# Moving the per-layer-embedding product of a hybrid block into its routing step, and unrolling the last stage

## The reference

```
h  = x + mixers(rmsnorm(x, g_mix)) @ w_out            # delta rule + convolution
h  = h + moe(rmsnorm(h, g_moe))                       # 64 experts in 8 groups, top 2, F = 256
gate = sigmoid(rmsnorm(h, g_ple) @ w_ple_gate)        # [T, D] @ [D, D]
h  = h + gate * (p @ w_ple_proj)                      # [T, 256] @ [256, D]
out = rmsnorm(h, g_final)
```

## Time and profile before

| | us |
|---|---|
| median of three runs (lowest, highest) | 1401.87 (1398.05, 1403.14) |
| the profiled execution's own time | 1394.22 |
| its span, first to last instruction | 1392.4 |
| PE busy in the span | 1149.8 (83%) |
| DVE busy | 623.1 (45%) |
| ACT busy | 314.4 (23%) |
| moved by DMA | 272.81 MB, 208 GB/s over the span |

### The profile page before, as it was taken

One profiled execution on the slowest core, in us unless ns is written; L12 is line 12 of the kernel. 1 busy time (PEld: TensorE's weight loads), 2 busy tenths in 40 slices (PEclk: granted clock), 3 DMA queues, 4 the chain that ended last, 5 costly groups with the idle time before them and its releaser, 6 DMA issues.

```text
span 1392.4 us, 17070 instructions
## 1 busy us (share of the span) xinstructions
PE 1149.8 (83%) x6357; PEld 761.7 (55%) x6358; DVE 623.1 (45%) x906; ACT 314.4 (23%) x685; POOL 248.3 (18%) x347
## 2 busy tenths in 40 slices
PE   6999899995888886998188878888887888838997
PEld 5888788874777775887033333323332333317775
DVE  5799899964745745322711111111111111154553
ACT  5212111134543434221010101001010000032232
POOL 4000100023564441000212111111211111011111
PEclk9999999997978998999589999999999988979998
DMA  6111121100000103211989999999799999961221
GB/s 200 31 46 32 51 55 46 46 1 0 2 1 1 62 2 114 92 64 57 368 324 425 424 424 421 418 409 383 316 421 424 424 423 415 374 241 55 99 98 45
DMA packets 68066, 272.81 MB, mean 196 GB/s; under 512 B 12521, under 2 KB 38314, under 8 KB 51370
## 3 DMA queue, kind: packets, MB, share of 16 engines
q1 hardware_dynamic: 56096, 254.33, 46.1%
q0 software_dynamic: 9456, 16.80, 3.2%
q10 hardware_dynamic: 2458, 0.92, 0.3%
HBM read 264.15 MB, written 25.43 MB: 208 GB/s over the span
## 4 chain that ended last, share of the span: by engine, by line
DMA 24%; PE 19%; DVE 3%; issue 2%; ACT 1%; SPq 1%; POOL 0%; POOLq 0%; ACTq 0%; DVEq 0%
DMA wup<-in_w_up_dram 20%; PE ps_u L2236 10%; PE ps_gate L94 5%; DMA qkvT<-in_w_ple_proj_dram 2%; PE ps_y L2257 2%; DMA xg<-xn_rows,gi 1%; PE ps_xg L2225 1%; PE ps_hT L2484 1%; PE ps_u L2280 1%; DMA convT<-y_rows 0%; DVE hn L2429 0%; DVE qkvT L2422 0%; DMA y_rows<-qkvT,si 0%; SPq L1707 0%; DVE hn L2453 0%
## 5 line engine op out<-in xcount | busy, mean ns | idle before, releaser
L2236 PE MATMUL ps_u<-wup,xgT 128*64 128x512 f32 x1024 | 259.1, 664 | 63.2 <-DMA wup<-in_w_up_dram 60.8
L2236 PEld LDWEIGHTS ps_u<-wup,xgT 128*64 128x64 f32 x1024 | 86.3, 152 | 234.7 <-issue 233.5
L94 PE MATMUL ps_b<-n_hi,wh 128*128 128x512 f32 x384 | 157.3, 410 | 0.6 <-DVE wl L418 0.6
L94 PE MATMUL ps_b<-n_lo,wh 128*128 128x512 f32 x384 | 151.8, 395 | 0.0
L94 PE MATMUL ps_b<-n_hi,wl 128*128 128x512 f32 x384 | 151.8, 395 | 0.0
L2156 DVE TENSOR_TENSOR hb<-sil,ps_u 128x256 f32<-128x256 f32 x32 | 13.5, 420 | 304.1 <-ACT sil L2096 304.1
L94 PEld LDWEIGHTS ps_b<-n_hi,wh 128*128 128x128 f32 x384 | 73.3, 191 | 16.5 <-issue 2.5
L94 PEld LDWEIGHTS ps_b<-n_hi,wl 128*128 128x128 f32 x384 | 73.0, 190 | 16.2
L94 PEld LDWEIGHTS ps_b<-n_lo,wh 128*128 128x128 f32 x384 | 73.1, 190 | 15.0 <-issue 1.0
L461 DVE SCALAR_TENSOR_TENSOR convT<-upad,vecT,convT 128x1024 f32<-128x1024 f32 (+1 forms) x75 | 79.6, 1061 | 0.0
L2096 ACT ACTIVATE sil<-ps_u 128x256 f32<-128x256 f32 x32 | 12.3, 383 | 291.7 <-PE ps_u L2236 291.7
(11 more groups left out here) (365 smaller groups left out, 1973.8 us busy)
## 6 DMA issues: line engine op xcount, KB each, us to landing
wup<-in_w_up_dram SPq DMA_DIRECT2D x64, 2048.0 KB, 18.6
zT<-in_w_down_dram SPq DMA_DIRECT2D x32, 1024.0 KB, 18.7
convT<-in_w_down_dram SPq DMA_DIRECT2D x32, 1024.0 KB, 19.9
wraw<-in_w_in_dram SPq DMA_DIRECT2D x24, 512.0 KB, 4.3
convT<-y_rows SPq DMA_DIRECT2D x16, 512.0 KB, 4.7
qkvT<-in_x_dram SPq DMA_DIRECT2D x8, 512.0 KB, 8.5
qkvT<-in_w_out_dram SPq DMA_DIRECT2D x8, 512.0 KB, 5.1
xr<-in_x_dram SPq DMA_DIRECT2D x8, 512.0 KB, 3.3
```

The source lines that it names most:

```text
L94: ins = nc.tensor.matmul(ps, lhs[a], rhs[b], start=first and k == 0, stop=last and k == 2)
L2236: last = nc.tensor.matmul(ps_u[k][HC[c], :], xgT[k][:, j, HC[c]], wup[k][c][:, j, :], start=j == 0, stop=j == NJ - 1)
```

## The change

1. **Loads.** In the output-product block SP, once `w_out` is split, also loads all of `p` (1 MB, to `qkvT` slots 10 and 11) and `w_ple_proj` (1 MB, slots 8 and 9).
2. **The product of p** is done in the routing block, in float32, without a split: two transposes and 2 x 2 matmuls of 512 columns for each of 8 tiles. It is laid around PE's three jobs: tiles 0 and 1 before `ps_tot`, tiles 2 to 4 and half of tile 5 before `ps_tab`, the rest after it. ACT copies each tile's turned rows and its result out of PSUM and stores the result (512 KB) to DRAM as `pp_rows`. Tiles 2 to 5 leave through `convT`, so SP waits for their stores before it fetches the second pair's down weights.
3. **End of the experts' block.** `w_ple_gate` alone is left (8 pieces). Five are split here; `silu` of pair 31 now comes before the third split on ACT, and `hidden(1)` and `hidden_turned(1)` before the third on DVE. The scatter of pair 31 and pieces 5 to 7 go to the final block. SP no longer waits for the scatters here; it fetches two tiles of `pp_rows`.
4. **Final block.** All 8 tiles are written out, without a loop. The product of `p` is gone; its rows come from `pp_rows`. Four tiles of experts' rows are asked for at the start, in two pairs of buffers, and tile t + 4 after that. On DVE `add_experts(t + 2)` stands right after `scale(t + 1)` at the step's start, and the output of tile t moves into the next step.

```diff
# output-product block, SP
+                sp.wait_ge(s_wo_lo, NJ)
+                sp.dma_start(p_all, p[0, 0].rearrange("(t q) d -> q t d", q=P)).then_inc(s_pin, 16)
+                sp.dma_start(wpp, w_ple_proj[0].rearrange("(j q) n -> q j n", q=P)).then_inc(s_pin, 16)
...
# routing block, SP
+                    if k:
+                        sp.wait_ge(s_pps, 16 * (NT - 4))
                     for c in G2:
                         fetch_down(sp, k, c, NPR * c + k)
...
# routing block, ACT
+                def p_out(t):
+                    act.wait_ge(e_pp, t + 1)
+                    nc.scalar.activation(ppo[t], ps_pp[t % 2][:].rearrange("p h n -> p (h n)"), ACT.Copy).then_inc(e_out, 1)
+                    act.wait_ge(e_out, t + 1)
+                    act.dma_start(pp_rows[t * P:(t + 1) * P, :], ppo[t]).then_inc(s_ppe if t < 2 else s_pps if t < NT - 2 else s_ppl, 16)
...
# routing block, PE
+                def p_half(t, h):
+                    for j in range(NJP):
+                        last = nc.tensor.matmul(ps_pp[t % 2][:, h, :], pT[t % 2][:, j, :], wpp[:, j, HF[h]], start=j == 0, stop=j == NJP - 1)
...
+                p_products(0, 2)
                 pe.wait_ge(s_iota, 9)
                 pe.wait_ge(s_rv, at["ohs"])
...
+                p_products(2, 5)
+                p_turn(6)
+                p_product(5)
                 pe.wait_ge(s_rv, at["onehots"])
...
+                p_half(5, 1)
+                p_products(6, NT)
...
# end of the experts' block, ACT (DVE alike)
                 result(0, p, 16 * i)
-                for j in range(2, N_X + 2):
+                silu(1, p + 1)
+                for j in range(2, N_E):
                     weights_high(j)
-                silu(1, p + 1)
                 result(1, p + 1, 16 * i)
-                for j in range(N_X + 2, NWJ):
-                    weights_high(j)
...
# final block, DVE
+                for j in range(N_E, NWJ):
+                    weights_low(j)
+                add_experts(0)
+                add_experts(1)
                 dve.wait_ge(s_gfin, 32)
+                scale(0)
+                low(0)
+                for t in range(NT):
+                    if t + 1 < NT:
+                        scale(t + 1)
+                    if t + 2 < NT:
+                        add_experts(t + 2)
+                    if t:
+                        scaled_out(t - 1)
+                    gated(t, 0)
+                    if t + 1 < NT:
+                        low(t + 1)
+                    gated(t, 1)
+                    add_gated(t)
+                scaled_out(NT - 1)
...
# final block, PE
+                    pe.wait_ge(f_lo, t + 1)
+                    product(t, 0)
+                    if t + 1 < NT:
+                        transposes(t + 1)
+                    product(t, 1)
...
# final block, SP
+                for t in range(NT + 1):
+                    if t + 4 < NT:
+                        sp.wait_ge(f_y2, t + 3)
+                        fetch_rows(sp, t + 4, t % 2)
+                    if t:
+                        sp.wait_ge(f_out, t)
+                        sp.dma_start(out[0, (t - 1) * P:t * P, :], ho[(t - 1) % 2]).then_inc(s_fo[(t - 1) % 2], 16)
+                    if t + 2 < NT:
+                        sp.wait_ge(f_m1, t + 1)
+                        fetch_ple(sp, t + 2, t % 2)
```

More of the change, by code:

```diff
@@ L2017, in _ @@
                 fetch_pairs(MID, NIT - 1)
-                for j in range(NWJ):
+                for j in range(N_E):
                     if j >= NRAW:
@@ L2393, in _, with gate @@
-                over_tiles(act, step)
+                    nc.scalar.activation(hx[t % 2][0][:], ps_h[:], ACT.Copy).then_inc(f_hi, 1)
+                def gate(t, h):
+                    act.wait_ge((f_g0, f_g1)[h], t + 1)
+                    nc.scalar.activation(hn[t % 2][:, HF[h]], ps_g[:, h, :], ACT.Sigmoid).then_inc((f_sg0, f_sg1)[h], 1)
+                for j in range(N_E, NWJ):
+                    weights_high(j)
+                square_ahead(0)
+                square_ahead(1)
+                high(0)
@@ L2402, in root @@
                     pool.wait_ge(ms, t + 1)
+                    if t >= 2:
+                        pool.wait_ge((f_hn, f_out)[n], t - 1)
                     nc.gpsimd.tensor_tensor(r8[n][g][:], s8[n][g][:], mh1[:], ALU.pow).then_inc(rs, 1)
[L2405 to L2413 removed]
+                scatter(pool, 1, slice(NPR - 1, NPR), 2 * NPR)
@@ L2512, in _, with product @@
-                over_tiles(pe, step)
+                def product(t, h):
+                    if t:
+                        pe.wait_ge((f_sg0, f_sg1)[h], t)
+                    x_ = hx[t % 2]
+                    for j in range(NJ):
+                        last = mm3(ps_g[:, h, :], [x_[0][:, j, :], x_[1][:, j, :]],
+                                   [wg[0][j][:, HF[h]], wg[1][j][:, HF[h]]], j == 0, j == NJ - 1)
+                    last.then_inc((f_g0, f_g1)[h], 1)
+                transposes(0)
```

322 lines of the change are left out of this document (156 added, 166 removed).

## The result

The kernel after takes **1376.16 us** (median of four runs, 1373.71 to 1378.89), the kernel before in the same rounds 1399.96 (four runs, 1396.20 to 1403.14). The ratio is **0.9857, 95% interval 0.9818 to 0.9896**: faster by 1.4%, a small gain but clear of the noise. The prediction was 1372.2, with a range from 1361 to 1387. The profiled execution took 1377.12 us, with a span of 1375.3.

A forecast was written before the change was run, and what follows sets the result against it. Experts' block bound by its weights, the rest mostly by PE or chains of waits. 1394.22 - 29.4 (final block) - 1.9 (end of experts' block) + 1.6 (routing) = 1364.5 profiled; median 7.65 higher, 1372.2 us, range 1361 to 1387.

The forecast's parts named there:

- Final block, pace: Final block: with p's work gone and adds reordered, PE sets 11.87 us steps; 96.8 us in place of 126.2, gain 29.4.
- DVE as the bound of the pace: Rival, final block: DVE or a root sets 13.5 us steps, gain only 16 us, about 1385; 15 in 100.
- The order of `silu`: End of experts' block: pair 31's silu and hidden rows ahead of splits let PE turn them 4.2 us sooner.
- The change of blocks: Experts' block to final block: the last scatter now stands behind this change, priced at 1.2 us.
- The cold turn: Start of final block: PE's first turn at the low clock takes 1.95 us in place of 0.87, +1.1.
- the thin cover: Start of final block: last three weight pieces split until 1242.5, tile 0's rows due about 1243; later pieces delay everything.
- Routing block: Routing block: p's product there costs 1.6 us in all, between -1 and +8, partly repaid by a warm PE.
- the rival's mechanism: Rival, routing block: gathers among stores and late weights, or a late clock, delay the experts' start 8 to 15 us; 12 in 100.
- The tables: Routing block: p's tiles on PE make `ps_tab` begin at 689.6, not 688.30, +1.3 us, delaying the gathers too.
- The half of a warm clock: Start of experts' block: PE arrives warm, saving some 3 us on first turn and product; half was counted.
- The low clock as a rival: Rival, routing block: low clock stays, tiles take 7.6 us, experts start up to 35 us later; 1418; 3 in 100.
- The sustained gap of 131 ns: Rival, final block: matmuls at this gap make a half 3.1 us, DVE sets pace near 10 us; 1357; 1 in 100.

The follow-up runs named there:

- e5_down: Kernel after with SP's wait for the stores of tiles 2 to 5 and the down weights behind it moved to the experts' block: 1371.83 us.
- e6_noproduct: Kernel after without p's turns, product and copies in the routing block; ACT stores other rows of the same size, output wrong: 1365.07 us.
- e10_nostore: Kernel after with p's product kept but without the pp_rows stores and their waits; final block reads another array, output wrong: 1362.37 us.
- e1_order: Kernel after with the old order of expert adds and output back in the final block, still without p's product there: 1408.96 us.
- e2_work: Kernel after with 12 more matmuls, unread, ahead of the first half of each final-block tile but the first: 1398.66 us.
- e4_scatter: Kernel after with the last scatter back in the experts' block, pieces 5 to 7 staying in the final block: 1374.79 us.
- e8_warm_routing: Kernel after with five useless float32 matmuls behind the last product of p in the routing block: 1382.71 us.
- c3_best: Kernel after with last scatter and piece 5 to 7 fetches in experts' block, later first pp_rows loads, 22 useless final-block matmuls: 1366.55 us, ratio 0.9769.

## Why the prediction was right, and where it was off

- **Final block, pace, -29.4 predicted, -27.5 measured.** The mechanism held: PE is busy for 98.60 of 98.70 us, and the chain has no DVE instruction between tiles. The step was sized 11.87 us from the 5.50 of a half and measured 12.08, since a half takes 5.60 to 5.62. 0.1 us over 15 halves and 0.2 on the first are the 1.9 us. Why the matmuls are 2% slower is open. It belongs to the new code and not to one execution: a half at full clock takes 5.60 to 5.62 us in e5_down, e6_noproduct and e10_nostore too, and their tiles took 97.4 to 97.9 us only because the first half was at 7.2 to 7.7 us. The splitting of the old pace into 12 matmuls' work and some 6 us of waits was true only of the old kernel. e1_order shows that the first couldn't be had without the order.
- **DVE as the bound of the pace** (a rival, 15 in 100) didn't come: e2_work, 84 matmuls for 19.4 us, says that there was no slack on PE and enough on DVE.
- **The order of `silu`, -4.2 predicted, -4.4 measured**: the mechanism held, and that the numbers meet is partly luck. PE's wait fell by 4.25 us, as I had it. But I had the down product as long as before or quicker, and at a clock of 0.50 it took 6.45 us in place of 4.78, so the last steps gained only 2.6 us. The other 1.8 us come from the pairs ahead of them, where nothing was changed and the kernels here differ by 5 us (507.5 to 512.8 from the first `silu` to the end of the last up product). In the other kernels with this order the last steps gained 3.8 to 4.1 us, which is what the term meant. Behind them, 1.4 us were lost again at the change of blocks, because the scatter of pair 30, issued at 1233.08, and not the last result is what the final block waits for.
- **The change of blocks, +1.2 predicted, is the step that failed by most** in its reasoning. I priced it as a thing of its own, between the 0.3 and 3.6 us of the earlier trace rows. It is the landing of POOL's last transfer plus 2.8 to 3.3 us, in thirteen kernels. The 3.6 us were such a landing themselves: the gather issued at 694.66 landed after 4.2 us, at 698.9, and the block began at 699.28. Here it made 3.1 us after the last result ended. The two loads of `pp_rows` beside it made that landing 2.6 us longer, a neighbour that the prediction hadn't counted. The cold turn took 1.98 us where 1.95 was said, but the kernel before had 1.08 at that place and not the 0.87 that I compared with. By parts: the scatter is issued 4.9 us behind the last result's copy in place of 1.9 (+3.0, where +1.2 was said); it takes 7.35 us in place of 6.07 (+1.3, where nothing was said); from its landing to tile 0's `scaled` it is 9.7 us in place of 10.1 (-0.4; the chain goes through tile 0's rows, 3.62 us, its additions, square and root, where it went through tile 1's rows, 6.55 us); and the turn has +0.9. Together the stage came to +4.6 where the sum had 1.2 + 1.1 = +2.3.
- **Pieces 5 to 7**: the thin cover was seen rightly. In the kernel after the splits ended at 1253.57, ahead of the rows at 1255.88; with the scatter moved (e4_scatter) they were on the chain.
- **Routing block, +1.6 predicted, +3.4 measured.** The start of the experts' block was said to be +3.1 and came at +3.2 (40.1 against 36.9 from the start of the logits' copy), but the reason was the wrong one, so that this match is luck. It isn't PE, ACT's last copy and the change: e6_noproduct, without the product, starts as late as after. It is the rival's mechanism, gathers among the stores, at 3 us where I gave it 8 to 15: they land 3 to 4 us later each, and e10_nostore, product in and stores out, starts at 36.8. The tables weren't 1.3 us late: a tile took 3.65 us with its turn where 3.88 was said, `ps_tot` and `ps_pre` ran at the full clock, and PE was done just as DVE's `r_sl` came at 695.12. The half of a warm clock that I counted, 1.5 us, didn't come: PE was idle for 4.70 us and stood at 0.50 at 714. By e8_warm_routing it wouldn't have been worth anything either, as DMA is full until 724.
- **The low clock as a rival, the side on which it is slower**, didn't come: the clock was 1.00 in the stretch at 676 and the tiles took 3.60 us.
- **The sustained gap of 131 ns** that the Trainium skill states in "TensorE: Matmul & The Clock Gate", section "Back-to-back issue gap", didn't come: 0.2335 us a matmul is farther from it than the row of before.

Off by 1.9, 1.8 and 2.3 us, all to one side, the sum was 5.7 us too low against the profiled stages. The medians of the same rounds say the same: they differ by 23.8 us where 29.7 was said. That 1376.16 is only 4 us above the predicted 1372.2 comes from the start, since the forecast began at a median of 1401.87 and these rounds have 1399.96.

## What to carry to other kernels

When two engines take turns as the bound, removing work from one and waits from the other doesn't give two gains that add: without the new order the same 84 matmuls less made the block slower, since they had filled the wait and kept TensorE's clock up. A block of the program that ends with a GpSimd transfer in flight ends when that transfer lands; keep other loads away from it, or issue it earlier, before you shorten the compute that seems to come last. And ask of each head start what sets the pace behind it: 2.9 us ahead of a stretch that is full of weights were worth nothing, 2.7 us ahead of one that PE sets stayed.

## What the runs showed of the hardware that I had not expected

- The next block began a fixed time after the landing of the last indirect transfer of the block before: 0.3 to 0.5 us at the experts' block, in thirteen kernels with landings between 4.2 and 8.0 us, and 2.8 to 3.3 us at the final block, in thirteen with landings between 3.3 and 8.6 us. That the change of blocks waits for it follows from this pattern; no run took the transfer away altogether, and why the rest differs between the two changes is open.
- A wait of 3.4 us between groups of dense matmuls brought the granted clock from 1.00 to 0.50 and cost some 1.5 us more in the group behind it; waits of up to 1.0 us in the kernel before left it at 1.00, and so did the 1.37 us ahead of the first turn in e10_nostore.
- The same two gathers at the end of the routing block took 4.2 and 5.6 us to land without the stores (4.4 in e10_nostore), where the DMA share was falling, and 7.1 to 9.8 us in the kernels with 512 KB stores, where it was 0.97 to 1.04 (after, e4_scatter, e6_noproduct, c3_best).
- The same code, up to the copy of the logits, ended between 657 and 672 us in different executions. At 480 to 500 the granted clock was 0.94 in the profile of before and 0.70 in that of after, and in nearly the same busy time, 14.4 and 14.7 us, PE got through 156 matmul records there and 81 here; why, is open. It is as large as many of the effects here, and the reason for comparing by stages.

```profile
480.00:500.00 20.00, 14.44 (x156) 13.47 (x158) 10.38 (x22) 8.94 (x29) 12.81 (x13) 0.94 0.01 1
```
```profile
480.00:500.00 20.00, 14.72 (x81) 13.96 (x79) 7.27 (x17) 6.46 (x24) 9.99 (x11) 0.70 0.00 1
```
